# First mLSTM tile's projection, samples' cache turns and samples' output stores moved across the attention-mLSTM stage boundary of a hybrid decoder layer

## The reference

```python
h = rms_norm(x, norm_mix_w)
q_a, k_a, v_a, q_m, k_m, v_m, o_m, gl = split_projection(h @ w_in)
# A: sliding-window attention, 8 q heads, 2 kv heads, head_dim 64, window 128, sinks
o_att = swa_prompt(q_a, k_a, v_a, sinks)                       # prompt
o_att, new_k, new_v = swa_sample(q_a, k_a, v_a, cache_k, cache_v, sinks)  # samples
# B: mLSTM, 4 heads, qk dim 64, v dim 128, running-max stabiliser
h_m, C, n, m = mlstm(q_m, k_m, v_m, ig, lf, C0, n0, m0, chunk)
o_ml = rms_norm(h_m, ml_norm_w) * sigmoid(o_m)
x = x + concat(o_att, o_ml) @ w_out
g, u = split(rms_norm(x, norm_ffn_w) @ w_ffn_in, 2)
x = x + (silu(causal_dwconv3(g)) * u) @ w_down
```

## Time and profile before

| | us |
|---|---|
| median of 3 runs (2567.98 to 2571.9) | 2569.51 |
| the profiled execution's own time | 2566.43 |
| its span in the trace | 2564.7 |
| PE busy | 2412.4 (94%) |
| DVE busy | 1630.4 (64%) |
| ACT busy | 907.5 (35%) |
| POOL busy | 914.8 (36%) |
| mean granted TensorE clock | 0.966 |

### The profile page before, as it was taken

How to read it: one execution, slowest core, us unless ns; L and a number is a source line. 1 busy time by engine, 2 the same in 40 slices (tenths; PEclk the granted TensorE clock), 3 DMA queues, 4 the chain that set the end, 5 groups by cost and what they waited for, 6 DMA issues and landing times.

```text
span 2564.7 us, 36591 instructions
## 1 busy us (share of the span) xinstructions
PE 2412.4 (94%) x13782; PEld 2192.9 (86%) x13782; DVE 1630.4 (64%) x2473; ACT 907.5 (35%) x1556; POOL 914.8 (36%) x724
## 2 busy tenths in 40 slices
PE   5999977999997699979999999999999999999999
PEld 4888866999996478868898888999999889999998
DVE  3666651656666534557777777666676876666765
ACT  2444441333333122343333353332333433333332
POOL 2332320222222004355544554343543544435441
PEclk9999977999998699989999999999999999999999
DMA  7222202111110435652222244222222442222121
GB/s 279 92 86 103 85 24 69 58 59 48 57 53 15 137 116 168 205 169 83 83 83 83 84 167 155 74 75 66 66 66 68 152 165 81 66 66 66 66 83 66
DMA packets 150102, 242.80 MB, mean 95 GB/s; under 512 B 17809, under 2 KB 113773, under 8 KB 147901
## 3 DMA queue, kind: packets, MB, share of 16 engines
q1 hardware_dynamic: 149649, 240.86, 27.8%
q10 hardware_dynamic: 288, 0.07, 0.0%
q0 software_dynamic: 32, 0.07, 0.0%
HBM read 185.08 MB, written 56.84 MB: 94 GB/s over the span
## 4 chain that ended last, share of the span: by engine, by line
PE 55%; DVE 3%; POOL 2%; DMA 2%; issue 2%; ACT 0%; SPq 0%; POOLq 0%; ACTq 0%; DVEq 0%
PE late_bank L2235 10%; PE late_bank L2236 10%; PE late_bank L2237 10%; PE late_bank L109 8%; PE late_bank L110 8%; PE late_bank L111 8%; DMA late_b_raw<-in_w_ffn_in_dram 2%; DVE late_t L2548 1%; PE late_bank L2176 1%; DVE late_gp L2536 0%; DVE late_acc L2562 0%; PE late_bank L2185 0%; POOL late_t_raw L2697 0%; DVE late_act_lo L2518 0%; DVE late_t_lo L2508 0%
## 5 line engine op out<-in xcount | busy, mean ns | idle before, releaser
L2536 DVE TENSOR_TENSOR late_gp<-late_bank,late_gp 128x384 f32<-128x384 f32 (+1 forms) x330 | 172.5, 523 | 328.0 <-PE late_bank L2237 327.8
L2235 PE MATMUL late_bank<-late_a_hi,late_b_hi 128*128 128x384 f32 (+1 forms) x1056 | 344.0, 326 | 14.8 <-DVE late_b_lo L2508 12.4
L2236 PE MATMUL late_bank<-late_a_lo,late_b_hi 128*128 128x384 f32 (+1 forms) x1056 | 342.9, 325 | 0.0
L2237 PE MATMUL late_bank<-late_a_hi,late_b_lo 128*128 128x384 f32 (+1 forms) x1056 | 341.9, 324 | 0.0
L2711 POOL TENSOR_TENSOR late_t<-late_t,late_gp 128x768 f32<-128x768 f32 (+1 forms) x66 | 132.1, 2019 | 512.9 <-DVE late_gp L2536 512.9
L109 PE MATMUL late_bank<-late_d_hi,late_act_hi 128*128 128x512 f32 (+1 forms) x724 | 283.3, 391 | 5.3 <-DVE late_acc L2562 4.6
L110 PE MATMUL late_bank<-late_d_lo,late_act_hi 128*128 128x512 f32 (+1 forms) x724 | 282.0, 390 | 0.0
L111 PE MATMUL late_bank<-late_d_hi,late_act_lo 128*128 128x512 f32 (+1 forms) x724 | 282.0, 390 | 0.0
L2235 PE MATMUL late_bank<-late_a_hi,late_t_hi 128*128 128x384 f32 (+1 forms) x792 | 260.3, 329 | 12.1 <-DVE late_gp L2536 10.1
L2562 DVE TENSOR_TENSOR late_acc<-late_bank,late_acc 128x512 f32<-128x512 f32 (+1 forms) x374 | 243.0, 681 | 34.5 <-PE late_bank L111 33.4
L2236 PE MATMUL late_bank<-late_a_lo,late_t_hi 128*128 128x384 f32 (+1 forms) x792 | 256.6, 324 | 0.0
(11 more groups left out here) (329 smaller groups left out, 5477.4 us busy)
## 6 DMA issues: line engine op xcount, KB each, us to landing
late_b_raw<-in_w_ffn_in_dram SPq DMA_DIRECT2D x66, 1024.0 KB, 5.1
late_d_raw<-in_w_down_dram SPq DMA_DIRECT2D x32, 1024.0 KB, 4.9
ml_hh<-h_parts SPq DMA_DIRECT2D x16, 1024.0 KB, 4.8
late_a_raw<-h_parts SPq DMA_DIRECT2D x14, 768.0 KB, 5.3
att_x<-in_x_prompt_dram SPq DMA_DIRECT2D x16, 512.0 KB, 3.6
h_parts<-att_h_hi SPq DMA_DIRECT2D x16, 512.0 KB, 2.7
h_parts<-att_h_lo SPq DMA_DIRECT2D x16, 512.0 KB, 3.4
late_o<-mixed SPq DMA_DIRECT2D x16, 512.0 KB, 4.8
```

The costliest lines, as they stand in the source:

```text
L2235: nc.tensor.matmul(out, w_h, hi[:, c, :], start=first, stop=False, skip_group_check=True)
L2236: nc.tensor.matmul(out, w_h, lo[:, c, :], start=False, stop=False, skip_group_check=True)
L2237: ins_ = nc.tensor.matmul(out, w_l, hi[:, c, :], start=False, stop=last, skip_group_check=True)
L2536: nc.vector.tensor_tensor(dst, bk, src, ALU.add).then_inc(c_dve, 1)
```

## The change

A new class `MlstmStart` holds what both stages now share, in semaphores and buffers that outlive the attention stage: the weight, the activations' buffer `hh` (placed over `h_hi` and `h_lo`), `z` (placed over `x`, `square`, `hn`, by a new order of the attention's buffers), the samples' output `os`, and the semaphores of load, projection and copy.

- SP, in the attention tail: the loads of tiles 0 and 1 of the mLSTM, ahead of the last two tiles' output stores.
- PE: the cache's turns and the samples' q and k turns come ahead of the last tile's `turn_p`; the four projection groups of mLSTM tile 0 stand in the tail, two behind the samples' scores, one behind the turns of the samples' weights, one behind the samples' PV.
- ACT: the samples' q copies ahead of `keep_p`; the four z copies at the end of the tail.
- DVE: the cache's copies and the first weight chunk ahead of the last tile's denominators (`keep_cache`), chunk 1 ahead of `keep_o`, chunk 2 ahead of the samples' scores, chunks 3 to 7 together behind their statistics.
- POOL: samples' keys go to a buffer of their own, `kn_s`; the wait for the k_prompt DMA is gone.
- The 16 stores of `os` are issued by SP in the mLSTM stage, behind the state loads, and waited for at its end.

```diff
+class MlstmStart:
+    def use_over(self, k, w_offset, h_offset, x_offset):
+        self.w.use_over(k, w_offset)
+        self.hh = k.nc.alloc_sbuf_tensor_at("att_next_hh", [P, 2, 2, D], F32R, offset=h_offset)
+        self.z = k.nc.alloc_sbuf_tensor_at("att_next_z", [P, 2, ML_W], F32, offset=x_offset)
+    def project(self, nc, pe, bank, g):
+        t = Tile(0, 0)
+        if g == 0:
+            self.h_in.wait(pe, t)
+        if g >= 2:
+            self.z_ready.wait(pe, t, g - 2)
+        for c in range(KC):
+            if g == 0:
+                pe.wait_ge(self.w.split, c + 1)
+            at, n = slice(c * P, (c + 1) * P), slice(g * ML_GW, (g + 1) * ML_GW)
+            ins_ = mm3(nc, bank[g % 2][:, 0:ML_GW], self.hh[:, 0, 0, at], self.hh[:, 0, 1, at],
+                       self.w.hi[:, c, n], self.w.lo[:, c, n], c == 0, c == KC - 1)
+        self.proj.mark(ins_)
@@ attention, SP
             tiles_loop(sp, period, 0, NT)
+            proj.wait(sp, samp)
+            h_out.wait(sp, samp)
+            h_out.wait(sp, samp - 1)
+            start.load_h(sp, h_dram, Tile(0, 0))
+            start.load_h(sp, h_dram, Tile(0, 1))
             store_o(Tile(0, NT - 2))
...
-            sp.wait_ge(s_os, 1)
-            store_os(sp, 0)
@@ attention, PE
-            turn_p(last)
-
+            pe.wait_ge(s_in, 32)
+            for b in range(2):
+                z_ready.wait(pe, samp, b)
+                for c in range(4):
+                    ins_ = nc.tensor.transpose(bank[b][:, c * P:(c + 1) * P], ck[:, b * 4 + c, :], C["ident"][:, :])
+                ins_.then_inc(sT_done, 1)
             qk_normed.wait(pe, samp)
...
+            turn_p(last)
             values(last)
...
             ins_.then_inc(s_score, 1)
+            start.project(nc, pe, bank, 0)
+            start.project(nc, pe, bank, 1)
...
             ins_.then_inc(s_turn, 1)
+            start.project(nc, pe, bank, 2)
...
             ins_.then_inc(s_pv, 1)
+            start.project(nc, pe, bank, 3)
@@ attention, ACT
-            act.wait_ge(s_os, 1)
-            store_os(act, 1)
+            for g in range(ML_G):
+                start.keep_z(nc, act, bank, g)
@@ attention, POOL
                     pool.dma_start(outs["k_prompt"][0, 0].rearrange("s k d -> s (k d)"), kn[:, :]).then_inc(k_out, 16)
-                    pool.wait_ge(k_out, 16)
@@ mlstm, SP
-            load_h(Tile(0, 0))
-            load_h(Tile(0, 1))
...
+            store_os(sp, o_dram, start)
...
+            sp.wait_ge(start.os_out, 16 * 16)
@@ mlstm, PE
-            for g in range(G):
-                project(Tile(0, 0), g)
@@ mlstm, ACT
-            for g in range(G):
-                keep_z(Tile(0, 0), g)
```

More of the change, by code:

```diff
@@ L49 @@
 IN_W = ATT_W + ML_W
+ML_G = 4
+ML_GW = ML_W // ML_G
 class Tile:
@@ L571, in _ @@
             last = Tile(0, NT - 1)
-            turn_p(last)
-            qk_normed.wait(pe, samp)
-            o_ready.wait(pe, last - 1)
-            for j in range(GQ):
-                ins_ = nc.tensor.transpose(bank[2][:, j * P:j * P + NS], qn[0:NS, j * P:(j + 1) * P], C["ident"][0:NS, 0:NS])
-            qk_turned.mark(ins_)
-            qk_turned.mark(nc.tensor.transpose(bank[3][:, 0:NS], kn[0:NS, :], C["ident"][0:NS, 0:NS]))
-            values(last)
             pe.wait_ge(s_in, 32)
@@ L587, in _ @@
                 ins_.then_inc(sT_done, 1)
+            qk_normed.wait(pe, samp)
+            o_ready.wait(pe, last - 1)
+            for j in range(GQ):
+                ins_ = nc.tensor.transpose(bank[2][:, j * P:j * P + NS], qn[0:NS, j * P:(j + 1) * P], C["ident"][0:NS, 0:NS])
+            qk_turned.mark(ins_)
+            qk_turned.mark(nc.tensor.transpose(bank[3][:, 0:NS], kn_s[:, :], C["ident"][0:NS, 0:NS]))
+            turn_p(last)
+            values(last)
             p_kept_v.wait(pe, last)
@@ L592, in _ @@
             pe.wait_ge(s_keep, 5)
+            pe.wait_ge(s_act, 1)
+            k_kept.wait(pe, samp)
             p_kept_a.wait(pe, last)
@@ L853, in period @@
                 softmax_stats(t, first=static and t.c == 0)
+                if static and t.c == NT - 1:
+                    keep_cache()
                 denominators(t)
@@ L1026, in mlstm @@
         bank = k.banks()
-        h_in = k.landed("h_in")
-        proj = k.steps("proj", G)
-        z_ready = k.steps("z_ready", G)
+        h_in, proj, z_ready = start.h_in, start.proj, start.z_ready
         turned = k.steps("turned", 2)
@@ L2794, in trunk_step @@
             ahead = Stage(nc, inner, "ahead")
[L2795 removed]
+            start = MlstmStart(ahead)
             w_in = ins["w_in"][0]
             def load_ml_w(sp):
[L2799 removed]
+                start.w.load(sp, [w_in[:, IN_W - 2 * MH:IN_W], w_in[:, ATT_W:IN_W - 2 * MH]])
             with ExitStack() as first_ctx:
```

95 lines of the change are left out of this document (57 added, 38 removed).

## The result

| | before | after |
|---|---|---|
| median, us | 2570.03 (2567.98 to 2571.9, 4 runs) | 2550.03 (2546.68 to 2554.65, 4 runs) |
| profiled execution, own time / span | 2566.43 / 2564.7 | 2554.65 / 2552.9 |
| mean granted TensorE clock | 0.966 | 0.97 |

The ratio is 0.9924, interval 0.9904 to 0.9943: faster by 20.0 us in the medians. (The median of before was 2569.51 us over the three runs known ahead; a fourth makes it 2570.03.) The forecast was 2547.2 us, 22.3 less than before. Two more measurements of the changed kernel, each with before on the same chip, gave 2550.94 against 2569.16 us, ratio 0.9929 [0.9916, 0.9942], and 2552.52 against 2570.92, 0.9926 [0.9911, 0.9941]: 18.2 and 18.4 us.

What follows compares the result with a forecast made beforehand. TensorE was taken as busy except at stage seams, with a 14.7 us wait for the mLSTM activations' DMA. 32.2 us off the path less 9.9 added gave 22.3: 2569.5 - 22.3 = 2547.2 us, range 2542.0 to 2558.0.

Steps and rivals of the forecast that it cites:

- The seam: From the last tile's last score matmul to the first mLSTM loop matmul; claimed 22.3 us less than before.
- seam's start to the end of `values`: Attention tail: `values` still limited by the exponentials' second half, start 367.5, length 6.86 us, bounds 1 us either way.
- to the end of group 0: First projection group in the tail, paced by DVE's weight subtractions of 1.72 us each, ending at 389.1.
- group 1: Second projection group, starting with PE cold and the clock rising under it: 6.4 us, ending at 395.5.
- turns: Eight transposes of the samples' weights on PE, at full clock: 1.0 us.
- PV: The samples' 64 small matmuls at full clock: 5.9 us from 11.3 at half clock, bounds 4.5 to 11.3.
- group 3: Last projection group, behind the samples' PV, at full clock: 4.2 us, ending at 410.9.
- copy and boundary: Last z copy (0.2 + 0.49) and the stage boundary (0.9, bound 2.0): 1.6 us together.
- Rival 1: Tail: the clock rises already under group 0; gain 25.0 us, 2544.5 us; chance 0.24.
- rival 3: Tail: the clock stays low to the stage's end; gain 6.1 us, 2563.4 us; chance 0.10 in whole or part.
- Rival 2: Tail: the clock never falls, cache turns shortening the hole before the exponentials; gain 29.3 us, 2540.2 us; chance 0.06.
- Rival 4: Next stage's SP queue: 16 stores delay tile 2's load, 15.7 us late; gain 6.6 us, 2562.9 us; chance 0.06.

Runs made afterwards that it cites:

- set C: Runs on one chip: before 2570.92 us, changed kernel 2552.52, changed kernel with DVE's subtractions moved earlier 2543.60, that plus PV spread through the last projection group 2548.58.
- set A: Runs on another chip: before 2569.16 us, changed kernel 2550.94, changed kernel with the projection back in the mLSTM stage 2556.59.
- the kernel with the spread PV: Changed kernel with eight of the samples' 64 PV matmuls behind each chunk of group 3: 2548.74 us, ratio 0.9920.
- the stores alone: Kernel before, with only the 16 stores of the samples' outputs moved to SP in the mLSTM stage: 2565.36 us, ratio 0.9985.

## Why the prediction was right, and by what errors

The seam was forecast at 78.8 - 22.3 = 56.5 us and measured at 60.4, 58.0 and 59.2; the median at 2547.2 and measured at 2550.0 to 2552.5, inside the range of 2542 to 2558. Little of that is luck: the terms that were too small come to 5.5 us and those that were too large to 1.6, so the errors did not cancel; they cost 3.9 of the 22.3 us. By the steps of the sum, on the first profile of after:

| step | forecast us | measured us |
|---|---|---|
| seam's start to the end of `values` | 18.5 | 17.8 |
| to the end of group 0 | 14.7 | 14.9 |
| group 1 | 6.4 | 5.7 |
| turns | 1.0 | 0.8 |
| group 2 | 4.2 | 4.4 |
| PV | 5.9 | 7.9 |
| group 3 | 4.2 | 6.6 |
| copy and boundary | 1.6 | 2.3 |

The second and third profiles have the same errors: PV 8.0 and 9.6, group 3 6.5 and 5.9. They are shorter in all because `values`, partly at full clock, ended 2.2 and 2.4 us sooner.

- **Start and `values`: the size was right, to 0.7 us; what limits it was not the second half of the exponentials.** That half ended at 362.23 in after. PE did the 16 turns of the probabilities in a row from 360.71, behind the samples' q and k turns, and came to the second half of them at 362.47 without a gap. It had started so late because the samples' turns, now ahead, waited for POOL (the 4.49 us); ahead of them `turn_p` could have started when the first exponentials ended, at 358.4. The exponentials' end would then have set the second half of the turns, by estimate 0.2 us sooner.
- **Group 0 paced by DVE: right,** in bursts 1.68 us apart (1.72 forecast). What the step missed is that DVE's idle time behind `values` could hold three of these subtractions. It stood in the trace of before:

```profile
374.63 0.69 DVE L789 TENSOR_TENSOR att_o<-att_bank,att_rden 128x512 f32<-128x512 f32 x1 [5.57 <-PE att_bank L528]
```

  Moving them gained 6.9 us of seam in set C, more than the moved projection itself (4.4 in set A).
- **Group 1 cold and the clock rising under it: right,** at 390.2. Rival 1, the rise already under group 0, happened from 376.5 to 379.9 and did not last; it did not decide.
- **PV: mis-sized, 7.9 for 5.9.** At full clock its rows are 0.227 apart for two matmuls, 0.1135 each, 7.3 for 64. The prediction had that figure at hand: `values` at full clock is 3.61 / 32 = 0.113 a matmul. It used the ratio of the two clocks, 0.53, on PV's cold 11.3 us, and that ratio does not carry over: PV cold is 0.176 a matmul, `values` cold 0.214. The remaining 0.6 us is the clock's fall near its end. The Trainium skill ("TensorE: Matmul & The Clock Gate", section "Wait — 56ns, not 53.3ns?") has a floor of about 62 ns a matmul, which would have made the PV an estimated 4.0 us; at 113.5 ns these matmuls are nowhere near it.
- **Group 3: the step that failed, 6.6 for 4.2.** "From here I take the full clock" did not hold: the clock fell at 403.8 within the PV. That is the part of rival 3 that came true, its price confined to group 3 and the last eleven matmuls of the PV (1.9 us at 0.176).
- **Copy and boundary: 2.3 for 1.6.** From the end of the z copy (413.01) to the first matmul of the loop it is 1.6 us; the earlier trace rows had 0.9 for the first boundary and the earlier trace rows 2.0 for this one. In the kernel with the spread PV it is 1.7 from DVE's last instruction.
- **Rival 2, a clock that never falls, did not come.** The cache's turns filled the first 1.1 us, the hole behind them was 4.49 us, and the clock fell at 359.5. The Trainium skill ("TensorE: Matmul & The Clock Gate", "Part 4: PE-mode transpose") would have it so, since by it transposes do not count as busy in the same way. The hole alone may have done it too, as it did in before, where the clock fell 2.7 us into a hole of 4.0 us without them; no run here tells these apart.
- **Rival 4, SP's queue: did not come.** The load of `n` was 3.5 us shorter and tile 2's load landed 1.8 us ahead of its use. The "cost it at nothing" was right for the reason given.

By parts, the experiments give a chain within one set. From before to the stores alone it is 8.5 us of seam and 3.8 of median; from there to the change without the projection 7.9 and 8.8 (the early load, 4.9 of idle time, and the new order of turns and chunks); from there to the whole change 4.4 and 5.7. That is 20.8 us of seam and 18.2 of median. The parts depend on each other: with the projection behind the PV, the stores would cost at most 2 us instead of 8.5.

## What to carry to other kernels

Fill a hole on the bounding engine only after asking what the filler itself waits for: here the projection waited for DVE, and putting DVE's work into DVE's own idle time gained more than the filler had. Compare seams step by step and with the clock beside each step: the gain of that edit looked like 5.8 us at group 0 beside one profile and was 3.4 to 4.2 beside profiles with nearly the same clock there. Price an instruction at another clock from the nearest row at that clock, per instruction, and not by the ratio of another instruction's two clocks. And follow the clock past the edit: a stretch rid of its cold time can be followed by a cold start of the next one, as in the three profiles with the spread PV, and a shorter seam is then not by itself a shorter program.
